# In each round of the softmax attentions, the query-key product is issued ahead of the transposes of older probabilities

## The reference, cut to what matters

```python
def diff_attention(q, k, v, lam):            # 4 heads, two maps (m = 0, 1) each, head dim 64
    ...
    logits = einsum('bqhmd,bkhmd->bhmqk', qi, k) * scale      # causal, softmax over keys
    p = softmax(logits); p = p[:, :, 0] - lam * p[:, :, 1]
    return einsum('bhqk,bkhe->bqhe', p, v)                    # v is 128 wide

def forgetting_attention(q, k, v, log_f):    # 8 heads, head dim 64
    ...
    logits = einsum('bqhd,bkhd->bhqk', qi, k) * scale + (c_i - c_k)   # causal
    return einsum('bhqk,bkhd->bqhd', softmax(logits), v)
```

## Time and profile before

| | |
|---|---|
| median of 3 runs | 2253.09 us (2251.55 to 2256.26) |
| the profiled execution, its own time | 2254.23 us |
| its span in the trace | 2252.4 us |
| TensorE busy over the span | 2149.5 us (95%) |
| VectorE / ScalarE / GpSimd busy | 768.0 / 742.9 / 846.3 us |
| granted TensorE clock over the execution | 0.983 of full |
| the two attentions | 171.2 to 257.2 us and 839.4 to 925.4 us of the span |

### The profile page before, as it was taken

How to read it: one execution, slowest core, us unless ns; L and a number is a source line. 1 busy time by engine, 2 the same in 40 slices (tenths; PEclk the granted TensorE clock), 3 DMA queues, 4 the chain that set the end, 5 groups by cost and what they waited for, 6 DMA issues and landing times.

```text
span 2252.4 us, 27470 instructions
## 1 busy us (share of the span) xinstructions
PE 2149.5 (95%) x10268; PEld 1760.5 (78%) x10268; DVE 768.0 (34%) x1445; ACT 742.9 (33%) x1231; POOL 846.3 (38%) x390
## 2 busy tenths in 40 slices
PE   7999999999999999999999999999788899999999
PEld 5886778888887877778888877877677677888887
DVE  5327442121013137341212023677576332221200
ACT  4236442222223136442222233544432334222221
POOL 3430134444434420234444434433344334444443
PEclk9999999999999999999999999999999999999999
DMA  6320023332333320023332322211111223333232
GB/s 190 103 84 1 11 78 109 99 96 94 101 87 94 93 75 1 29 85 98 98 93 93 98 70 75 66 57 48 47 47 38 64 76 112 94 101 95 89 103 70
DMA packets 138736, 178.21 MB, mean 79 GB/s; under 512 B 19857, under 2 KB 87697, under 8 KB 138641
## 3 DMA queue, kind: packets, MB, share of 16 engines
q1 hardware_dynamic: 137024, 175.25, 25.8%
q10 hardware_dynamic: 1616, 1.64, 0.2%
HBM read 174.76 MB, written 2.10 MB: 79 GB/s over the span
## 4 chain that ended last, share of the span: by engine, by line
PE 85%; DVE 7%; issue 5%; ACT 2%; POOL 1%; DMA 0%; POOLq 0%; ACTq 0%; SPq 0%; DVEq 0%
PE PS L1340 24%; PE PS L1342 24%; PE PS L1341 24%; PE PS L1547 3%; PE PS L1559 2%; DVE R L1252 1%; PE PS L1714 1%; POOL w_lo L505 1%; PE PS L1535 1%; PE PS L1346 1%; PE PS L1486 1%; PE PS L1621 1%; PE PS L1650 1%; DVE R L1247 1%; DVE X L1106 0%
## 5 line engine op out<-in xcount | busy, mean ns | idle before, releaser
L505 POOL TENSOR_TENSOR w_lo<-R,w_hi 128x1024 fp32r<-128x1024 f32 (+1 forms) x268 | 629.9, 2352 | 908.4 <-ACT w_hi L580 908.3
L580 ACT ACTIVATE w_hi<-R 128x1024 fp32r<-128x1024 f32 (+1 forms) x268 | 278.3, 1041 | 949.0 <-PE PS L1342 935.8
L1340 PE MATMUL PS<-xt_hi,w_hi 128*128 128x512 f32 x1120 | 446.1, 398 | 3.4 <-DVE xt_lo L924 3.4
L1342 PE MATMUL PS<-xt_hi,w_lo 128*128 128x512 f32 x1120 | 438.3, 391 | 0.0
L1341 PE MATMUL PS<-xt_lo,w_hi 128*128 128x512 f32 x1120 | 438.1, 391 | 0.0
L1340 PE MATMUL PS<-w_hi,xt_hi 128*128 128x512 f32 x928 | 382.1, 412 | 12.2 <-DVE xt_lo L924 9.7
L1342 PE MATMUL PS<-w_hi,xt_lo 128*128 128x512 f32 x928 | 365.7, 394 | 0.0
L1341 PE MATMUL PS<-w_lo,xt_hi 128*128 128x512 f32 x928 | 365.2, 394 | 0.0
L1340 PEld LDWEIGHTS PS<-xt_hi,w_hi 128*128 128x128 f32 x1120 | 211.8, 189 | 47.7 <-issue 5.3
L1342 PEld LDWEIGHTS PS<-xt_hi,w_lo 128*128 128x128 f32 x1120 | 211.6, 189 | 44.5
L1341 PEld LDWEIGHTS PS<-xt_lo,w_hi 128*128 128x128 f32 x1120 | 211.9, 189 | 43.7 <-issue 1.0
(11 more groups left out here) (231 smaller groups left out, 2228.2 us busy)
## 6 DMA issues: line engine op xcount, KB each, us to landing
R<-in_w_in SPq DMA_DIRECT2D x48, 512.0 KB, 3.7
R<-in_w_gate SPq DMA_DIRECT2D x88, 256.0 KB, 2.8
R<-in_w_up SPq DMA_DIRECT2D x88, 256.0 KB, 3.0
raw<-in_w_in SPq DMA_DIRECT2D x44, 512.0 KB, 3.6
R<-in_w_down SPq DMA_DIRECT2D x40, 512.0 KB, 3.8
R<-in_w_ffn_gate SPq DMA_DIRECT2D x44, 256.0 KB, 2.8
R<-in_w_ffn_up SPq DMA_DIRECT2D x44, 256.0 KB, 3.1
R<-in_w_ffn_down SPq DMA_DIRECT2D x20, 512.0 KB, 3.8
```

Of the source, the lines that this page charges most:

```text
L505: nc.gpsimd.tensor_tensor(w_lo[:, r, 0:subs, :], raw_of(stage)[:, r, 0:subs, :], w_hi[:, r, 0:subs, :].bitcast(F32), ALU.subtract).then_in ...
L580: nc.scalar.activation(w_hi[:, r, 0:subs, :], raw_of(stage)[:, r, 0:subs, :], ACT.Copy).then_inc(hi_ready, 1)
L1340: mm(out_, a_hi, b_hi, start=start, stop=False)
L1342: return mm(out_, a_lo, b_hi, start=False, stop=stop)
```

## The change

In each round u of TensorE's loop, the block that issues the query-key product of unit u is moved ahead of the block that issues the transposes of unit u-5. The order within a round was transposes (u-5), query-key (u), value product (u-6); it is now query-key (u), transposes (u-5), value product (u-6). No instruction is added or removed, no wait changes its semaphore or value, and the loops of the other engines are as they were.

```diff
                 for u in range(len(units1) + PRODUCT):
+                    if u < len(units1):
+                        kind, (h, m), i = units1[u]
+                        ...
+                        if b + u >= 4:
+                            pe.wait_ge(exp_done, b + u - 3)
+                        mm(PS[:, u % 4, 0:upto], q, kk, start=True, stop=False)
+
+                        mm(PS[:, u % 4, upto - P:upto], ident_b[:, :], causal_b[:, :], start=False, stop=True).then_inc(s_mm, 1)
                     v = u - TURN
                     if 0 <= v < len(units1) and has_output[v]:
                         i = units1[v][2]
                         ...
                         last.then_inc(pt_mm, 1)
-                    if u < len(units1):
-                        kind, (h, m), i = units1[u]
-                        ...
-                        mm(PS[:, u % 4, 0:upto], q, kk, start=True, stop=False)
-
-                        mm(PS[:, u % 4, upto - P:upto], ident_b[:, :], causal_b[:, :], start=False, stop=True).then_inc(s_mm, 1)
                     v = u - PRODUCT
                     if v >= 0 and has_output[v]:
```

More of the change, by code:

```diff
@@ L1523, in attention1 @@
                 for u in range(len(units1) + PRODUCT):
+                    if u < len(units1):
+                        kind, (h, m), i = units1[u]
+                        tok, upto = slice(i * P, (i + 1) * P), P * (i + 1)
+                        if kind == "diff":
+                            q, kk = QAT[m][:, h, tok], KAT[:, h, 0:upto]
+                        else:
+                            q, kk = QBT[0:66, h, tok], KBT[0:66, h, 0:upto]
+                        if b + u >= 4:
+                            pe.wait_ge(exp_done, b + u - 3)
+                        mm(PS[:, u % 4, 0:upto], q, kk, start=True, stop=False)
+                        mm(PS[:, u % 4, upto - P:upto], ident_b[:, :], causal_b[:, :], start=False, stop=True).then_inc(s_mm, 1)
                     v = u - TURN
```

## The result

In a paired measurement of 20 runs each the changed kernel has a median of 2256.36 us (2255.05 to 2260.61), the kernel before 2253.12 us (2248.37 to 2257.17). The ratio is 1.0016, 95% interval 1.0009 to 1.0023. So it is slower, by 2.0 to 5.2 us, and by less than the 0.2% that the prediction had named as what a measurement can tell from no change (the interval here is 0.07% to either side); the forecast was 2254.5 us, range 2249 to 2259.

What follows compares the result with a forecast made beforehand. TensorE was taken as the bound, busy 82.1 of 86.0 us in an attention. Terms +0.96, +0.10, -0.06 and -0.28 gave +0.72 for one attention, +1.4 for both: 2254.5 us against 2253.09, range 2249.0 to 2259.

Steps and rivals of the forecast that it cites:

- The wait of 0.76: TensorE's wait in each differential head, ahead of the two-block value product, for ScalarE's copy-out; claimed to stay.
- A head is 0.32 us longer: Differential part: value products wait for later copy-outs, so the next head is 0.32 us later; three full heads give +0.96.
- The walk of the prediction: Step-by-step timing of one differential head from the value product at 188.13, giving the next head 0.32 us later.
- Differential half with its entry: Three full differential heads, +0.96 us, and the entry into forgetting units, +0.1, in one attention.
- Forgetting half with its end: Forgetting part: changed joints sum to -0.06 us, and the earlier last copy-out gives -0.28, in one attention.
- a query-key product behind a 65-wide value product: Forgetting part: joint not in the trace, taken as 0.055 us, 25 times, +1.38; bounds 0 and 0.11.
- the 0.055: Extra us a product pays behind a mask, taken also for query-key behind a value product in the forgetting part.
- (b): Rival: query-key weights load beside the value product ahead, third part -1.43 us, total 2251.7 us; chance 0.10.
- (c): Rival: weight load stands bare behind each value product, 0.19 us, total 2264.7 us; chance 0.11.
- The end of the attention: Last query-key product starts sooner, its copy-out comes 0.28 us sooner, and the last wait of 0.37 nearly goes: -0.28.
- Rival (a): TensorE's waits for copy-outs vanish in both attentions, gain 6.4 us, total 2246.7 us; chance 0.07.
- the rest merely shift: Outside the attentions: what follows starts when the last division is done and shifts with it.

## Why the prediction was right

In the attention the mechanism held point by point, and so did the numbers behind it: +0.72 us forecast, +0.77 measured. That the two halves were off in opposite directions, by +0.13 and -0.06, made the sum look a little better than its parts.
- The wait of 0.76 stays: right. It is 0.81, and its chain from the mask of the odd round (187.23) to the value product (189.31) takes 2.08 us, as before (186.05 to 188.13).
- A head is 0.32 us longer: 9.85 against 9.51, so 0.34. The walk of the prediction and the rows agree: from the value product that waits to the next, 2.12 against 2.10 predicted, and to the third, 4.88 against 4.86.
- Differential half with its entry: 1.06 predicted, 1.19 in the kernel with that half alone.
- Forgetting half with its end: -0.34 predicted, -0.40 measured. The term that I could not see in the trace of before, a query-key product behind a 65-wide value product, is in these rows of the changed kernel:

```profile
250.24 0.33 PE L1559 MATMUL PS<-R 128*128 128x65 f32 x2
...
250.41 1.08 PE L1533 MATMUL PS<-R 66*128 66x512 f32 x2
...
251.32 0.22 PE L1535 MATMUL PS<-causal_b,ident_b 128*128 128x128 bf16 x1
```

The value product of one block takes 0.17, as it did ahead of transposes, and the query-key product of size 4 takes 0.91 up to its mask, where it took 0.86 behind transposes (193.72 in the earlier trace rows, its mask at 194.58): the 0.055 that I had taken from the mask. Rivals (b), 0, and (c), 0.19, are both out. The rule of the Trainium skill behind (b) ("TensorE: Matmul & The Clock Gate", Part 2: What happens when you issue a matmul) holds behind a 128-wide product (0.86 us for size 4 from 195.19 to its mask at 196.05, behind a value product) and leaves 0.055 bare behind one of 65 columns.
- The end of the attention: the value product of four blocks starts 0.36 us behind the transposition ahead of it (253.18, 253.54), where it took 0.64 (251.30, 251.94), so 0.28 less, as predicted; TensorE's rows show no wait there any more.
- Rival (a) is out: the waits did not vanish.

What the sum did not hold is the stretch outside: 1.44 us forecast, 3.2 us between the medians, of which the attentions are 1.54. I let the rest merely shift, and the kernel with fifteen extra transposes shows that a shift is not always free of effect there. That the total fell into the range all the same is luck in this part: the range was set by other terms. A range for a change this small has to carry the rest too, some 3 us each way by the kernels here.

And one thing was read too narrowly, though it did not change the forecast. I saw one wait per head and one cause. There was a second limit close behind it, the join, through only 0.10 us ahead of the copy-out in the trace of before. With the value product a round later this limit is what TensorE waits for, and the edit that I had priced as a loss of 0.72 us is a gain of 2.75.

## What to carry to other kernels

When two blocks in an engine's queue change places, one producer gets cover and another loses it. Work out the lead of each against the chain that it feeds (transposes, copy-out, value product here; exponential, join, transposes there) before deciding, since the same swap was worth +0.8, -6.6, -2.8 and -0.2 us an attention in four settings of the leads. Behind a wait that recurs in every period another chain may end nearly as late; look what else is through only just in time, lengthen the lead of the first and look again. Where buffers allow it, longer leads beat the order: with a round more for the join and two for the copy-out each attention takes 4.1 us (new order) and 4.0 us (old order) less than in the kernel before. The value product a round later together with the new order takes 3.7 us off it without another buffer of probabilities.

## What was not expected of the hardware

- The attention stretches repeat to 0.02 us between executions and layers, while the whole kernel has a spread of 5 to 11 us between executions of one program (where there are eleven or more). With TURN = 4 in the new order, twelve runs fall into two groups: 2243.7 to 2246.6 us at a mean granted clock of 0.988 to 0.989, and 2250.8 to 2253.7 us at 0.984 to 0.985.
- Fifteen extra transposes ahead of each attention, 3.3 us of work on the busiest engine, cost 0.0002 of the time (-0.0008 to 0.0011), and the granted clock was higher with them: 0.989 in six of its eleven runs, against 0.981 to 0.986 in the kernel before.
- A value product that had waited for its copy-out cost 0.04 to 0.05 us more than its passes. Its weight loads start together with it, not ahead of it (the kernel before):

```profile
188.13 0.52 PEld L1559 LDWEIGHTS PS<-R 128*128 128x128 f32 x4 [0.99 <-ACT R L699]
```
